# Outputs of two attention heads in the two halves of one PSUM bank, evicted together

## The chip, the cores and the metric

The kernel runs on one core of a Trainium2 chip. The metric is the device time of one execution in microseconds (us). The kernel before takes 481.25 us, the median of 3 runs (481.04 to 482.96). The kernel after is measured in the same way.

## The reference

One decoder layer on x of 256 tokens by 1024 channels, in float32, with a condition vector c:

```
mod = silu(c) @ w_ada + b_ada                      # 1024 -> 6 x 1024: sh1, sc1, g1, sh2, sc2, g2
h = rms_norm(x, g_pre_mix) * (1 + sc1) + sh1
proj = h @ w_in                                    # q, k, v of 16 heads, index heads, gates
o_sb = stick_breaking_attention(q, k, v)           # 6 heads of 64
o_mb = moba_attention(...)                         # 5 heads: at 256 tokens a causal softmax with ALiBi
o_ds = dsa_attention(...)                          # 5 heads: the 64 best keys of each query by an indexer
g = sigmoid(gate_logits + b_gate)
y = (g_sb * (o_sb @ w_proj_sb) + g_mb * (o_mb @ w_proj_moba) + g_ds * (o_ds @ w_proj_dsa)) @ w_o
x = x + g1 * rms_norm(y, g_post_mix)
h = rms_norm(x, g_pre_ffn) * (1 + sc2) + sh2
y = (silu(gate) * up) @ w_down                     # SwiGLU, 2816 wide
x = x + g2 * rms_norm(y, g_post_ffn)
```

For a head, with scores z of 256 queries by 256 keys, softmax heads form exp(z - max) / sum and stick-breaking heads exp(z + sums over later keys of log(1 - sigmoid(z))), both causal, and multiply the result with v. That product is 64 channels by 256 tokens.

## The kernel before, in words

**Precision.** The large products are made of two cuts of each operand: a high part (`whi`, `hhi`, `ohi`: ScalarE copies the float32 value to fp32r) and the rest (`wlo`, `hlo`, `olo`: VectorE subtracts the high part). `three` issues high*high, high*low and low*high (L1198 to L1200). So each weight that arrives by DMA in `raw` is cut by ScalarE (L611) and then by VectorE (L877) before TensorE uses it.

**The unit loop.** The product of h with `w_in` is divided into 51 units, numbered u = 0 to 50, by `mix_units`. A unit is one TensorE accumulation over 8 chunks of 128 channels into bank 0 or 1 (`unit`), taken out by ScalarE (`take_unit`). Units 27 to 50 are gates. Units of one weight block share its cuts: units 27 to 30 are block 11, 31 to 34 block 12, 35 to 38 block 13, and so on. A block is cut in quarters, listed in `PIECES_AT` at the units of the block before.

Everything else of the stage is hung on unit numbers. Each engine runs the same loop over u, and at each u the steps that are due, in program order. Semaphores join the engines. For head n (0 to 4 moba, 5 to 10 stick-breaking, 11 to 15 dsa):

- `SCORES_AT`, unit 13 + 2n: TensorE makes z. The two heads of a pair are made together (`TOGETHER_AT`), a pair being heads 0-1, 2-3, 5-6, 7-8, 9-10, 11-12, 13-14. Heads 4 and 15 are single.
- `EXP_AT`, one unit later: for a softmax head the exponential on ScalarE; for a stick-breaking head three ScalarE steps (L710 to L712), one on VectorE (L1037) and a triangular mask on GpSimd (L551).
- `NORM_AT`, two units later: VectorE normalises a softmax head.
- `SECOND_AT`, three units later (`second`): a softmax head's probabilities are turned by TensorE into bank 4 (`B_T`); for a stick-breaking head the sums over later keys are added to z, ScalarE takes the exponential into `buft` (L748) and GpSimd masks it (L543).
- `OUTPUT_AT`: TensorE multiplies `buft` with v (`output`). Heads with even number within their branch land on PSUM partitions 0 to 63, odd ones on 64 to 127. ScalarE writes `ohi` (L740), VectorE the rest (L1015).

**Other work in the loop.** `LOGITS_AT` are the indexer's logits (units 5 to 12) in banks 2 to 5. `ROUND_AT` (units 25 to 32) are VectorE's 8 rounds of top-8. The modulation rows 1 and 2 (`w_ada`) come by GpSimd's DMAs, VectorE multiplies and adds them up (`accumulate`, L946), TensorE sums over partitions (`sum_acc`) and turns the row (`turn_rows`), and VectorE forms columns (`columns`, which ends with an increment of `col_ready`, L933): group 1 at units 24, 25 and 26, group 2 at units 48, 49 and 50.

**PSUM banks before.** 0 and 1: units. 2 to 5: logits and scores (`z_place`: heads 0 to 4 in 2 and 3; stick-breaking heads h in 2 + h % 4, so that head 8 is in bank 5; dsa heads in 5, 4, 2, 3, 2). 4: turned probabilities. 5 (`B_ADA`): modulation sums and the indexer's turned weights. 6 and 7 (`B_O`): outputs, bank 6 + n % 2. The turned sums of groups 0, 1, 2 are in banks 7, 5, 4 (`B_ROWS`).

**After the loop.** Each branch's output is projected, gated by VectorE, added up by GpSimd (L581, L584), cut, multiplied with `w_o`, normalised, and then the SwiGLU stage runs over 11 steps of 256 hidden channels. The order of all this is written out by hand; no planner is involved.

Of the kernel before, what the change touches and what calls it, by code (L numbers as in the profile page):

```python
# [19 lines left out]
F32 = mybir.dt.float32  # L20
F32R = mybir.dt.float32r
ALU = mybir.AluOpType
ACT = mybir.ActivationFunctionType
AX_X = mybir.AxisListType.X

P = 128
D = 1024
KC = D // P
S = 256
# [213 lines left out]
def decoder_layer(nc, x, c, w_ada, b_ada, g_pre_mix, g_post_mix, w_in, b_gate, w_proj_sb,  # L243
                  w_proj_moba, w_proj_dsa, w_o, g_pre_ffn, g_post_ffn, w_up, w_down, out):
    ctx = ExitStack()
    with ctx:
# [74 lines left out]

        psum = ctx.enter_context(nc.psum_tensor("psum", [P, 8, BANK], F32))
        bank = [psum[:, i, :] for i in range(8)]
        B_UNIT, B_Z, B_T, B_ADA, B_O = 0, 2, 4, 5, 6
        B_ROWS = (7, B_ADA, B_T)
        B_Y = ((6, 0), (4, 6))
        B_TURNED = (2, 4)
        B_UP = ((2, 3), (0, 1))
# [264 lines left out]
        def _(act):  # L593
# [103 lines left out]
            for u in range(N_UNITS):  # L697
# [23 lines left out]
                if u in EXP_AT and EXP_AT[u] in SOFT_NO:  # L721
# [12 lines left out]
                                             scale=SLOPES[2 * h + (branch == "ds")],  # L734
                                             bias=smax[:, n % 2, t:t + 1], accum_out=ssum[:, n % 2, t:t + 1])
                    ins.then_inc(exp_ready, 1)
                for n in OUTPUT_AT.get(u, ()):
                    p0, ch = HD * (HEADS[n][1] % 2), O_CHUNK[HEADS[n][0]][HEADS[n][1]]
                    act.wait_ge(o_ready, n + 1)
                    act.activation(ohi[p0:p0 + HD, ch, :], bank[B_O + n % 2][p0:p0 + HD, 0:S], ACT.Copy).then_inc(o_hi, 1)  # L740
                if u in SECOND_AT:
                    n = SECOND_AT[u]
                    if n >= 2:
# [114 lines left out]
        def _(dve):  # L858
# [56 lines left out]
            def columns(g):  # L915

                dve.wait_ge(m_turned, g + 1)
                m, first, second = col[g][:, :], col[g][:, 0:KC], col[g][:, KC:2 * KC]
                bias = VEC_ADA + 2 * KC * g
                turned_sums = bank[B_ROWS[g]][:, :].rearrange("p (c j r) -> p j c r", c=4, j=4)[:, :, :, 0]  # L920

                then(dve.tensor_tensor(m.rearrange("p (j c) -> p j c", j=4), vecs[:, bias:bias + 2 * KC].rearrange("p (j c) -> p j c", j=4),
                                       turned_sums, ALU.add if g == 0 else ALU.subtract))

                if g == 0:
                    ins = dve.scalar_tensor_tensor(second, second, 1.0, vecs[:, VEC_PRE_MIX:VEC_PRE_MIX + KC], ALU.add, ALU.mult)
                elif g == 1:
                    ins = dve.tensor_tensor(first, first, vecs[:, VEC_POST_MIX:VEC_POST_MIX + KC], ALU.mult)
                else:
                    then(dve.scalar_tensor_tensor(first, first, 1.0, vecs[:, VEC_PRE_FFN:VEC_PRE_FFN + KC], ALU.add, ALU.mult))  # L930
                    ins = dve.tensor_tensor(second, second, vecs[:, VEC_POST_FFN:VEC_POST_FFN + KC], ALU.mult)
                then(ins)
                dve.sem_inc(col_ready, 1)  # L933
# [54 lines left out]
            for u in range(N_UNITS):  # L988
# [7 lines left out]
                if u in LOGITS_AT:  # L996
# [5 lines left out]
                    for t, (c0, c1) in enumerate(((0, P), (P, CAUSAL))):  # L1002
# [4 lines left out]
                            ins = dve.scalar_tensor_tensor(score[:, c0:c1], bufp[h % 2][:, c0:c1], w, score[:, c0:c1],  # L1007
                                                           ALU.mult, ALU.add)
                        ins.then_inc(score_added, 1)
                for n in OUTPUT_AT.get(u, ()):  # L1010
                    p0, ch = HD * (HEADS[n][1] % 2), O_CHUNK[HEADS[n][0]][HEADS[n][1]]
                    dve.wait_ge(o_hi, n + 1)

                    lo = olo[p0:p0 + HD, ch, :] if ch < FULL_OCH else ohi[HD:P, ch, :]
                    dve.tensor_tensor(lo, bank[B_O + n % 2][p0:p0 + HD, 0:S],  # L1015
                                      ohi[p0:p0 + HD, ch, :].bitcast(F32), ALU.subtract).then_inc(o_lo, 1)
                if u in NORM_AT and NORM_AT[u] in SOFT_NO:

                    n = NORM_AT[u]
# [175 lines left out]
        def _(pe):  # L1195
# [38 lines left out]

            def turn_rows(g):
                pe.wait_ge(m_ready, g + 1)
                if g == 2:
                    pe.wait_ge(pt_ready, N_SOFT)
                for n in range(4):
                    mm = pe.transpose(bank[B_ROWS[g]][:, P * n:P * (n + 1)], mrow[:, P * n:P * (n + 1)], ident[:, :])  # L1240
                mm.then_inc(m_turned, 1)

            def spread_gain(i):
# [59 lines left out]
            def scores(together):  # L1303
                for n in together:
                    m = Z_BEFORE[n]
                    if m is None:
                        pe.wait_ge(relu_ready, H_IX)
                    elif m in SB_NO:
                        pe.wait_ge(a_ready, SB_NO[m] + 1)
                    else:  # L1310
                        pe.wait_ge(max_ready, SOFT_NO[m] + 1)
                    if z_place(n) == B_T:
                        pe.wait_ge(pt_ready, softs_before(SB_FIRST))
                    elif z_place(n) == B_ADA:
                        pe.wait_ge(col_ready, 2)
                made = []
                for n in together:
                    _, h, tq, tk, _ = HEADS[n]
# [23 lines left out]
            def output(heads):  # L1342

                for n in heads:
                    if n in SB_NO:
                        pe.wait_ge(a_masked, 2 * (SB_NO[n] + 1))
                    else:
                        pe.wait_ge(pt_ready, SOFT_NO[n] + 1)
                    if n >= 2:
                        pe.wait_ge(o_lo, n - 1)  # L1350
                for keys in range(2):
                    for n in heads:
                        h, v0 = HEADS[n][1], HEADS[n][4]
                        p0, a = HD * (h % 2), buft[n % 2]
                        dst, cols = bank[B_O + n % 2][p0:p0 + HD, :], slice(v0 + HD * h, v0 + HD * (h + 1))
                        if keys == 0:
                            pe.matmul(dst[:, 0:S], v[:, 0, cols], a[:, 0:S], start=True, stop=False, skip_group_check=True)  # L1357
                        else:
# [11 lines left out]
            for u in range(N_UNITS):  # L1370
# [12 lines left out]
                if u in LOGIT_PAIR_AT:  # L1383
                    j = LOGIT_PAIR_AT[u]
                    if j == 0:
                        pe.wait_ge(unit_read, 5)
                        pe.wait_ge(vec_ready, 1)
                    if j == 1:
                        pe.wait_ge(wix_ready, 1)
                    if j >= 2:  # L1390
                        pe.wait_ge(relu_ready, 2 * (j - 1))
                    query_major([(bank[B_Z + h % 4], qk[:, T_QIX + h // 2, :], qk[:, T_KIX, :], HD * (h % 2))
# [183 lines left out]
```

## Time and profile before

| | |
|---|---|
| median of 3 runs | 481.25 us |
| the profiled execution | 479.4 us |
| its span (first to last instruction) | 477.7 us |
| mean granted TensorE clock | 0.988 of full speed |
| TensorE matmuls busy | 443.4 us, 93% |
| VectorE busy | 325.6 us, 68% |
| ScalarE busy | 242.8 us, 51% |
| GpSimd busy | 58.5 us, 12% |
| DMA | 98.79 MB, mean 207 GB/s |

The profile is one execution, seen by the hardware profiler. Its durations and gaps belong to its own 479.4 us, not to the median. A busy share is a mean over stages that have different limits: the head of the kernel, up to 30 us, waits for DMA; the unit loop lasts until about 225 us; the merge of the branches until about 262 us; the rest is the product with `w_o` and the SwiGLU stage. Matmuls are pipelined, so a row's duration is longer than the distance to the next row's start.

### The profile page before, as it was taken

The numbers are of one execution on the slowest core, as the hardware profiler recorded it, in microseconds if no ns is written. First come the engines' busy times: TensorE is split into PE (matmuls) and PEld (weight loads), VectorE is DVE, ScalarE is ACT, GpSimd is POOL, SyncE is SP. The second block draws the span as 40 slices with busy tenths as digits, with TensorE's granted clock in tenths as the row PEclk, the third lists the DMA queues.
The fourth block names the chain that finished last, engine by engine and source line by source line (L and its number), as shares of the span: only waits on it lengthen the run. The fifth ranks groups of instructions, "written<-read, shape, count | busy, mean of one in ns | idle before, by whom it ended". The sixth has DMA issues, their size and how long they took to land.

```text
span 477.7 us, 7668 instructions
## 1 busy us (share of the span) xinstructions
PE 443.4 (93%) x2933; PEld 388.9 (81%) x2933; DVE 325.6 (68%) x529; ACT 242.8 (51%) x426; POOL 58.5 (12%) x96
## 2 busy tenths in 40 slices
PE   0959999999989998999998899999999999999994
PEld 0529999999978998998987699888888888888883
DVE  2047678879599969793789656786855775595545
ACT  5046546556666755757457337653544253344332
POOL 2001002100024130002587200000000000000000
PEclk9959999999999999999999999999999999999999
DMA  8997897597865574742656920898475556630002
GB/s 302 424 357 221 296 326 239 181 325 248 282 232 169 218 265 150 266 159 66 200 188 240 365 88 1 281 363 273 142 247 190 169 182 184 236 107 0 2 0 88
DMA packets 56369, 98.79 MB, mean 207 GB/s; under 512 B 5036, under 2 KB 41492, under 8 KB 53268
## 3 DMA queue, kind: packets, MB, share of 16 engines
q1 hardware_dynamic: 54036, 81.62, 49.7%
q0 software_dynamic: 2304, 16.78, 10.0%
q8 instruction: 19, 0.31, 0.3%
q14 instruction: 10, 0.08, 0.1%
HBM read 97.35 MB, written 1.05 MB: 206 GB/s over the span
## 4 chain that ended last, share of the span: by engine, by line
PE 77%; DMA 6%; DVE 6%; ACT 4%; issue 3%; POOL 2%; SPq 1%; DVEq 0%; ACTq 0%; POOLq 0%; PEldq 0%
PE psum L1508 16%; PE psum L1198 15%; PE psum L1200 14%; PE psum L1199 14%; PE psum L1509 8%; DMA ada_end<-in_w_ada_dram 4%; PE psum L1472 3%; DVE wlo L877 3%; DMA raw<-in_w_o_dram 2%; ACT whi L611 2%; PE psum L1357 1%; PE psum L1294 1%; PE psum L1292 1%; POOL xn L584 1%; PE psum L1328 1%
## 5 line engine op out<-in xcount | busy, mean ns | idle before, releaser
L1508 PE MATMUL psum<-hcut,whi 128*128 128x512 f32 x320 | 111.8, 394 | 0.0
L1198 PE MATMUL psum<-hcut,whi 128*128 128x256 f32 (+1 forms) x360 | 105.8, 294 | 4.0 <-DVE hcut L981 2.7
L877 DVE TENSOR_TENSOR wlo<-raw,whi 128x1024 fp32r<-128x1024 f32 (+4 forms) x92 | 91.7, 1026 | 22.2 <-ACT whi L611 21.9
L1199 PE MATMUL psum<-hcut,whi 128*128 128x256 f32 (+1 forms) x360 | 102.2, 284 | 0.0
L1200 PE MATMUL psum<-hcut,wlo 128*128 128x256 f32 (+1 forms) x360 | 102.2, 284 | 0.0
L1509 PE MATMUL psum<-hcut,wlo 128*128 128x256 f32 x320 | 88.8, 278 | 0.0
L611 ACT ACTIVATE whi<-raw 128x1024 fp32r<-128x1024 f32 (+4 forms) x92 | 74.3, 842 | 17.6 <-DMA raw<-in_w_in_dram 15.6
L1198 PEld LDWEIGHTS psum<-hcut,whi 128*128 128x128 f32 (+1 forms) x360 | 68.8, 191 | 9.0 <-issue 4.3
L1508 PEld LDWEIGHTS psum<-hcut,whi 128*128 128x128 f32 x320 | 60.0, 188 | 14.1 <-issue 0.2
L1199 PEld LDWEIGHTS psum<-hcut,whi 128*128 128x128 f32 (+1 forms) x360 | 69.0, 192 | 0.0
L1200 PEld LDWEIGHTS psum<-hcut,wlo 128*128 128x128 f32 (+1 forms) x360 | 68.8, 191 | 0.0
L1509 PEld LDWEIGHTS psum<-hcut,wlo 128*128 128x128 f32 x320 | 60.1, 188 | 0.3
L1127 DVE TENSOR_TENSOR dlo<-draw,dhi 128x2048 fp32r<-128x2048 f32 x11 | 25.1, 2292 | 44.1 <-ACT dhi L786 44.1
L1122 DVE TENSOR_TENSOR wlo<-raw,whi 128x1024 fp32r<-128x1024 f32 x40 | 47.1, 1221 | 4.5 <-ACT whi L779 4.5
L779 ACT ACTIVATE whi<-raw 128x1024 fp32r<-128x1024 f32 x40 | 39.8, 1047 | 3.1 <-PE psum L1509 3.1
L786 ACT ACTIVATE dhi<-draw 128x2048 fp32r<-128x2048 f32 x11 | 20.9, 1911 | 31.2 <-PE psum L1200 31.2
L824 ACT ACTIVATE fsil<-fsil 128x256 f32<-128x256 f32 x20 | 8.4, 418 | 52.8 <-DVE fsil L1139 52.8
L946 DVE SCALAR_TENSOR_TENSOR acc<-xn,csil,acc 128x2048 f32<-128x2048 f32 x14 | 32.9, 2352 | 3.2 <-DMA xn<-in_w_ada_dram 3.1
L1198 PE MATMUL psum<-dhi,fhi 128*128 128x512 f32 x88 | 34.5, 392 | 0.0
L1200 PE MATMUL psum<-dhi,flo 128*128 128x512 f32 x88 | 34.4, 391 | 0.0
L1199 PE MATMUL psum<-dlo,fhi 128*128 128x512 f32 x88 | 34.3, 389 | 0.0
L1198 PE MATMUL psum<-whi,hcut 128*128 128x320 f32 (+2 forms) x80 | 28.6, 358 | 3.2 <-issue 2.2
(169 smaller groups left out, 692.1 us busy)
## 6 DMA issues: line engine op xcount, KB each, us to landing
raw<-in_w_up_dram SPq DMA_DIRECT2D x22, 1024.0 KB, 7.6
xn<-in_w_ada_dram POOLq DMA_DIRECT2D x16, 1024.0 KB, 5.2
raw<-in_w_in_dram SPq DMA_DIRECT2D x7, 2048.0 KB, 9.4
draw<-in_w_down_dram SPq DMA_DIRECT2D x11, 1024.0 KB, 5.1
raw<-in_w_in_dram SPq DMA_DIRECT2D x4, 1280.0 KB, 7.1
raw<-in_w_in_dram SPq DMA_DIRECT2D x3, 1536.0 KB, 7.2
raw<-in_w_ada_dram SPq DMA_DIRECT2D x2, 2048.0 KB, 9.6
ada_end<-in_w_ada_dram SPq DMA_DIRECT2D x4, 1024.0 KB, 16.8
```

The source lines that it names most:

```text
L611: act.activation(block_view(whi[b % 2], b)[0:p, chunks, cols], block_view(raw[r % 2], b)[0:p, chunks, cols], ACT.Copy).then_inc(w_hi, 1)
L779: act.activation(block_view(whi[slot], B_FFN)[:, 2 * q:2 * q + 2, :], block_view(raw[slot], B_FFN)[:, 2 * q:2 * q + 2, :], ACT.Copy).then_ ...
L786: act.activation(dhi[slot][:, :, :], draw[slot][:, :, :], ACT.Copy).then_inc(d_hi, 1)
L877: dve.tensor_tensor(block_view(wlo[b % 2], b)[0:p, chunks, cols], block_view(raw[r % 2], b)[0:p, chunks, cols], block_view(whi[b % 2], b)[ ...
L946: ins = dve.scalar_tensor_tensor(acc[:, :], ada_part, csil[:, k:k + 1], acc[:, :], ALU.mult, ALU.add)
L1122: dve.tensor_tensor(block_view(wlo[slot], B_FFN)[:, 2 * q:2 * q + 2, :], block_view(raw[slot], B_FFN)[:, 2 * q:2 * q + 2, :], block_view(w ...
L1127: dve.tensor_tensor(dlo[slot][:, :, :], draw[slot][:, :, :], dhi[slot][:, :, :].bitcast(F32), ALU.subtract).then_inc(d_lo, 1)
L1198: pe.matmul(dst, a[0], b[0], start=first, stop=False)
L1199: pe.matmul(dst, a[0], b[1], start=False, stop=False)
L1200: return pe.matmul(dst, a[1], b[0], start=False, stop=last)
L1508: pe.matmul(dst[:, :], wh, hcut[:, k, :, :].rearrange("p a s -> p (a s)"), start=k == 0, stop=False)
L1509: mm = pe.matmul(dst[:, S:2 * S], wl, hhi[:, k, :], start=False, stop=k == KC - 1)
```

## The change

The outputs of both heads of a pair go to bank 6, the even head to partitions 0 to 63 and the odd one to 64 to 127, as before within each bank. One ScalarE instruction and one VectorE instruction then handle 128 partitions. Single heads (4 and 15) keep 64 partitions. TensorE's `output` waits once for `o_lo` of all heads ahead. Bank 7, no longer an output bank, becomes `B_ADA`: modulation sums, the indexer's turned weights and all turned sums are there. Bank 5 holds logits and scores alone, and the waits that guarded its double use are gone.

```diff
-        B_UNIT, B_Z, B_T, B_ADA, B_O = 0, 2, 4, 5, 6
-        B_ROWS = (7, B_ADA, B_T)
+        B_UNIT, B_Z, B_T, B_O, B_ADA = 0, 2, 4, 6, 7
...
-                for n in OUTPUT_AT.get(u, ()):
-                    p0, ch = HD * (HEADS[n][1] % 2), O_CHUNK[HEADS[n][0]][HEADS[n][1]]
-                    act.wait_ge(o_ready, n + 1)
-                    act.activation(ohi[p0:p0 + HD, ch, :], bank[B_O + n % 2][p0:p0 + HD, 0:S], ACT.Copy).then_inc(o_hi, 1)
+                if u in OUTPUT_AT:
+                    heads = OUTPUT_AT[u]
+                    parts, ch = HD * len(heads), O_CHUNK[HEADS[heads[0]][0]][HEADS[heads[0]][1]]
+                    act.wait_ge(o_ready, heads[-1] + 1)
+                    act.activation(ohi[0:parts, ch, :], bank[B_O][0:parts, 0:S], ACT.Copy).then_inc(o_hi, len(heads))
...
-                turned_sums = bank[B_ROWS[g]][:, :].rearrange("p (c j r) -> p j c r", c=4, j=4)[:, :, :, 0]
+                turned_sums = bank[B_ADA][:, :].rearrange("p (c j r) -> p j c r", c=4, j=4)[:, :, :, 0]
...
-                for n in OUTPUT_AT.get(u, ()):
-                    p0, ch = HD * (HEADS[n][1] % 2), O_CHUNK[HEADS[n][0]][HEADS[n][1]]
-                    dve.wait_ge(o_hi, n + 1)
-
-                    lo = olo[p0:p0 + HD, ch, :] if ch < FULL_OCH else ohi[HD:P, ch, :]
-                    dve.tensor_tensor(lo, bank[B_O + n % 2][p0:p0 + HD, 0:S],
-                                      ohi[p0:p0 + HD, ch, :].bitcast(F32), ALU.subtract).then_inc(o_lo, 1)
+                if u in OUTPUT_AT:
+                    heads = OUTPUT_AT[u]
+                    parts, ch = HD * len(heads), O_CHUNK[HEADS[heads[0]][0]][HEADS[heads[0]][1]]
+                    dve.wait_ge(o_hi, heads[-1] + 1)
+
+                    lo = olo[0:parts, ch, :] if ch < FULL_OCH else ohi[HD:P, ch, :]
+                    dve.tensor_tensor(lo, bank[B_O][0:parts, 0:S], ohi[0:parts, ch, :].bitcast(F32),
+                                      ALU.subtract).then_inc(o_lo, len(heads))
...
                 pe.wait_ge(m_ready, g + 1)
-                if g == 2:
-                    pe.wait_ge(pt_ready, N_SOFT)
                 for n in range(4):
-                    mm = pe.transpose(bank[B_ROWS[g]][:, P * n:P * (n + 1)], mrow[:, P * n:P * (n + 1)], ident[:, :])
+                    mm = pe.transpose(bank[B_ADA][:, P * n:P * (n + 1)], mrow[:, P * n:P * (n + 1)], ident[:, :])
...
                     if z_place(n) == B_T:
                         pe.wait_ge(pt_ready, softs_before(SB_FIRST))
-                    elif z_place(n) == B_ADA:
-                        pe.wait_ge(col_ready, 2)
...
                         pe.wait_ge(pt_ready, SOFT_NO[n] + 1)
-                    if n >= 2:
-                        pe.wait_ge(o_lo, n - 1)
+                if heads[0]:
+                    pe.wait_ge(o_lo, heads[0])
...
-                        dst, cols = bank[B_O + n % 2][p0:p0 + HD, :], slice(v0 + HD * h, v0 + HD * (h + 1))
+                        dst, cols = bank[B_O][p0:p0 + HD, :], slice(v0 + HD * h, v0 + HD * (h + 1))
...
-                    if j == 1:
-                        pe.wait_ge(wix_ready, 1)
```

## Rows read from the trace of the kernel before

**Rows 1.** The page's chain that ended last: shares of the span by engine.

```profile
PE 77%; DMA 6%; DVE 6%; ACT 4%; issue 3%; POOL 2%; SPq 1%; DVEq 0%; ACTq 0%; POOLq 0%; PEldq 0%
```

**Rows 2.** TensorE's waits, 140 to 225 us: who <- for whom: total us, times, longest.

```profile
PE psum L1198 <- DVE wlo L877: 0.7, 1, 0.7
PE psum L1339 <- DVE smax L1052: 0.6, 1, 0.6
PE psum L1357 <- POOL buft L543: 0.6, 1, 0.6
```

**Rows 3.** TensorE's timeline: start, us, line, out<-in, count, idle before and releaser.

```profile
138.87 0.70 PE L1298 MATMUL psum<-qk 64*128 64x256 f32 x4 [1.86 <-DVEq L933]
```

**Rows 4.** VectorE's timeline, 138 to 149 us.

```profile
138.50 0.17 DVE L928 TENSOR_TENSOR col<-col,vecs 128x8 f32<-128x8 f32 x1
...
141.39 1.22 DVE L877 TENSOR_TENSOR wlo<-raw,whi 128x1024 fp32r<-128x1024 f32 x1
142.53 0.55 DVE L1037 SCALAR_TENSOR_TENSOR bufp<-psum,bufa 128x384 f32<-128x384 f32 x1
...
144.43 2.40 DVE L946 SCALAR_TENSOR_TENSOR acc<-xn,csil,acc 128x2048 f32<-128x2048 f32 x1
146.75 1.30 DVE L877 TENSOR_TENSOR wlo<-raw,whi 128x1024 fp32r<-128x1024 f32 x1
148.52 0.88 DVE L1015 TENSOR_TENSOR olo<-psum,ohi 64x256 fp32r<-64x256 f32 x2 [0.47 <-ACT ohi L740]
```

**Rows 5.** GpSimd's masks, the output waiting for one, VectorE beside the last.

```profile
137.02 0.54 POOL L551 TENSOR_SCALAR_AFFINE_SELECT bufp<-bufp 128x128 f32<-128x128 f32 x2 [0.71 <-DVE bufp L1037]
144.39 2.59 POOL L543 TENSOR_SCALAR_AFFINE_SELECT buft<-buft 128x128 f32<-128x128 f32 x2 [6.83 <-ACT buft L748]
147.23 0.65 PE L1357 MATMUL psum<-buft,v 128*64 128x256 f32 x4 [0.62 <-POOL buft L543]
...
160.00 0.55 DVE L1037 SCALAR_TENSOR_TENSOR bufp<-psum,bufa 128x384 f32<-128x384 f32 x1
160.37 0.53 POOL L543 TENSOR_SCALAR_AFFINE_SELECT buft<-buft 128x128 f32<-128x128 f32 x2 [0.58 <-ACT buft L748]
```

**Rows 6.** The chain in order of time: output of heads 7 and 8.

```profile
162.57 0.58 PE psum L1357 x4
```

**Rows 7.** Timeline: VectorE's last quarter of block 12, and TensorE reaching it.

```profile
150.86 1.22 DVE L877 TENSOR_TENSOR wlo<-raw,whi 128x1024 fp32r<-128x1024 f32 x1
...
154.04 0.28 PE L1198 MATMUL psum<-hcut,whi 128*128 128x256 f32 x1
```

**Rows 8.** Instructions of lines 740, 1015, 656: duration ns min/median/max, starts.

```profile
L740 ACT ACTIVATE ohi<-psum x16: 365/379/382, 105.3 to 219.7; 64x256 fp32r<-64x256 f32 x16
L1015 DVE TENSOR_TENSOR olo<-psum,ohi x14: 406/422/428, 105.7 to 209.7; 64x256 fp32r<-64x256 f32 x14
L656 ACT ACTIVATE qk<-psum x18: 371/385/386, 41.5 to 118.7; 128x256 f32<-128x256 f32 x18
```

**Rows 9.** Timeline after the output of heads 9 and 10.

```profile
179.09 0.88 DVE L1015 TENSOR_TENSOR olo<-psum,ohi 64x256 fp32r<-64x256 f32 x2 [1.02 <-ACT ohi L740]
...
182.34 0.52 PE L1339 MATMUL psum<-ident,bufp 128*128 128x128 f32 x3 [0.63 <-DVE smax L1052]
...
185.75 0.36 PE L1198 MATMUL psum<-hcut,whi 128*128 128x256 f32 x1 [0.74 <-DVE wlo L877]
```

**Rows 10.** Column tiles: a pair, the modulation sums, the single head; one record's duration.

```profile
118.55 0.65 PE L1357 MATMUL psum<-buft,v 128*64 128x256 f32 x4
...
217.83 1.06 PE L1231 MATMUL psum<-acc,neg 128*32 128x512 f32 x8
218.83 0.65 PE L1357 MATMUL psum<-buft,v 128*64 128x256 f32 x2
...
L1231 PE MATMUL psum<-acc,neg x16: 592/605/617, 123.3 to 218.3; 128*32 128x512 f32 x16
```

**Rows 11.** The chain in order of time: the load of `w_o`.

```profile
242.12 8.71 DMA raw<-in_w_o_dram
```

## The prediction

> **What bounds the kernel now.** I read the chain of waits first. TensorE holds 77% of it and VectorE 6% [rows 1]: the kernel is a sequence of matrix products, and another engine matters only where TensorE stands still for it. So the second view is the list of TensorE's own waits in the stage that the change touches, the mixer's unit loop (60 to 225 us of the span). Between 140 and 225 us it has three entries: 0.7 us for `wlo`, 0.6 us for `smax`, 0.6 us for `buft` [rows 2]. Ahead of them is a longer one, the product at 138.87 us, idle 1.86 us before, released by VectorE's sequencer at L933 [rows 3]. L933 is `sem_inc(col_ready)`, the end of `columns(1)`. Third, I read the timelines of VectorE and GpSimd around these four places, since TensorE can only gain where both are early enough.
>
> **Part 1: bank 5 is free of modulation sums.** Before, bank 5 held the summed modulation row of group 1, and scores of heads 7 and 8 (one of them in bank 5) waited in `scores` until `columns(1)` had run. The last of its instructions stands at 138.50 us [rows 4], and TensorE goes on at 138.87 [rows 3]. After, sums and turned sums live in bank 7, which no scores use, and the wait is gone. What else do these scores wait for? The index heads' relu and the softmax heads' `pt_ready`, both many units old; so they can follow unit 27 at once. Gain: 1.86 us. Below that lies zero, if another operand of unit 28 or of `second(6)` is late. Unit 28 uses the weight block of unit 27, already cut. `second(6)` needs GpSimd's mask of `bufp`, which starts at 137.02 and takes 0.54 us [rows 5]; `second(6)` now comes after scores and unit 28, which end well after 140 us. Neither holds it. I take 1.86 us.
>
> The other waits that the diff takes out (the logits' wait for `wix_ready`, `turn_rows(2)`'s for the last `pt_ready`, the scores' wait for head 11) show no idle time of TensorE anywhere in the lists, so they are worth nothing. `turn_rows`, `rows` and `columns` keep their instructions and only change banks; their order against each other is kept by `m_ready` and `col_ready` as before. No DMA is added, removed or moved in program order.
>
> **Part 2: what the earlier TensorE meets.** Everything after 138.87 us now comes 1.86 us earlier on TensorE, and ScalarE follows it, because its waits there are for TensorE. VectorE does not: it has hardly a gap up to its 0.47 us wait at 148.52 us [rows 4].
>
> First, the mask of `buft` for head 6, on which TensorE's output of heads 5 and 6 waited 0.62 us [rows 5]. Its two instructions began at 144.39 and took 2.59 us, while the same two began at 160.37 and took 0.53 us [rows 5]. The difference is what VectorE ran: a 2.40 us L946 from 144.43 with two SBUF tensors in [rows 4], against L1037 from 160.00, which reads PSUM and one SBUF tensor [rows 5]. Moved by 1.86 us, the mask begins at 142.53. There VectorE ends the L877 of 141.39 (1.22 us, until 142.61) and then runs L1037 (142.53 in the record) and the top-8 work until 144.43 [rows 4], none of which takes two SBUF tensors. So the mask should be done by about 143.2, and TensorE wants it at 147.23 - 0.62 - 1.86 = 144.75. The wait goes: 0.62 us more. If the mask stays 2.59 us long it keeps the whole wait: zero. It would become worse only if it slid behind a second long VectorE instruction. I take 0.62, and say openly that it is a matter of 1.3 us of phase.
>
> The Trainium skill (SBUF — State Buffer, "Who interferes with whom") says that a VectorE instruction with two SBUF inputs contends with a GpSimd instruction that reads SBUF, and one with at most one SBUF input, outside the two-port modes, doesn't. The trace agrees, 2.59 against 0.53 us; without the rule the mask's length would be chance, and the sum would be 0.62 us smaller.
>
> Second, the same contention can now hit the mask for head 8: it moves from 160.37 to 157.89, where VectorE is in accumulation and cutting. At the worst length seen near, 2.59 us, it ends at 160.48, and the output of heads 7 and 8 wants it at 162.57 [rows 6] - 2.48 = 160.09. That costs up to 0.4 us, at best nothing; I take nothing, since the row of 2.59 us began at the very start of a long instruction.
>
> Third, VectorE's cuts. TensorE's first unit of weight block 12 reaches the last quarter at 154.04 us [rows 7], after the change at 151.56. VectorE cuts that quarter in the L877 of 150.86 [rows 7]. It comes 0.47 us earlier because ScalarE's `ohi` is no longer late, and 0.44 us earlier by part 3, so it ends at 149.95 + 1.22 = 151.17. It fits by 0.4 us. Here a small new wait is nearest.
>
> **Part 3: two evictions become one, seven times.** Seven pairs of heads had two ScalarE copies of 64x256, 0.379 us each, and two VectorE subtractions, 0.422 us each [rows 8]. A ScalarE copy of 128x256 takes 0.385 us [rows 8], so the full height costs no more than half of it; VectorE's one I take at its 64x256 time, with 0.35 and 0.6 us as wide bounds. ScalarE gets back 7 x 0.37 = 2.6 us and VectorE 7 x 0.42 to 0.46 = 3.1 us, but in time of engines that are not the bound. It reaches TensorE where the chain runs through them: after the output of heads 9 and 10. There L1015 starts at 179.09 and takes 0.88 us for two; behind it in VectorE's order stand the normalisation, L1048, L1050 and L1052, for which the transposes at 182.34 waited 0.63 us, and then one accumulation and the L877 for which unit 39 waited 0.74 us at 185.75 [rows 9]. One subtraction less starts both 0.46 us earlier. The first wait shrinks from 0.63 to 0.17; the second stays 0.74, as TensorE and VectorE both come 0.46 earlier. Gain 0.46 us, not 0.92. With a 0.6 us subtraction it is 0.28 us. The other six pairs save nothing on TensorE beyond part 2, as no wait stands behind them.
>
> What speaks against merging is that ScalarE's copy of the first head no longer overlaps the wait for the second. Both heads' products end together already (four records of L1357 in 0.65 us), so that costs under 0.1 us of ScalarE.
>
> **Part 4: two heads write one bank.** The output products of a pair run on two column halves of the array. Pair: four records in 0.65 us; the single last head: two records, also 0.65 us [rows 10]. So halves run side by side now, in different banks. In one bank the nearest rows are the modulation sums, four column tiles of bank 5: eight records of 605 ns in 1.06 us [rows 10]; one after the other they would take 4.8 us. I take zero. The other end is a full single-head output more for each pair, 0.65 + about 0.2 us, 7 times: 5.6 us. The waits on `o_lo` ask for all heads ahead, as before: heads 5 and 6 are written at 147.23 [rows 5] and read until 149.40 [rows 4], the next pair is written at 162.57 [rows 6]. The alternation of two banks hid nothing.
>
> **Sum.** -1.86 - 0.62 - 0.46 = -2.9 us. Does it survive to the end? After 190 us no wait of TensorE stands in the list [rows 2]. The next stage is a chain of ScalarE, VectorE and GpSimd with the 8.71 us load of `w_o` that starts at 242.12 [rows 11], and each link is released by the one before, the load too (VectorE's cut frees its buffer), so the whole chain moves. The feed-forward part is TensorE's. The profiled execution took 479.4 us (span 477.7 and 1.7 around it), so it becomes 476.5. It was 1.85 us faster than the median shown; against 481.25 I predict 478.3 us.
>
> **Rivals.**
> A. Only the bank wait goes, and phases of VectorE and GpSimd take back the rest (the mask stays blocked, or block 12's last quarter is late): -1.9 + up to 0.3, about 479.5 us. For it: VectorE is full there, margins are 0.4 and 1.3 us. Against: both margins come out positive.
> B. The time goes into new waits almost wholly: unit 31, the mask of head 8, then unit 35 wait for a VectorE that was the true bound between 126 and 167 us. About -0.5 us, 480.8. For it: VectorE's 0.47 us gap is its only one for 20 us. Against: TensorE waited for none of its cuts there, with 2 us of room.
> C. More than forecast: VectorE's relief and unblocked masks also shorten the 0.74 us wait at 185.75. -3.7 us, 477.5.
> D. Slower: two column halves in one bank don't run side by side. Place: L1357 and L1359 in all seven pairs; +5.6 - 2.9 = +2.7 us, 484.0. It decides as soon as a pair costs 0.42 us more than now. Against it the 1.06 us of the sums; for it only that these use explicit 32-wide tiles.
>
> **Chances.** Forecast 0.50, A 0.22, B 0.12, C 0.10, D 0.06. Within 0.5% (2.4 us, about what a measurement tells from no change) begins at 478.85. The forecast lies 0.55 us under it, so I give it three quarters for faster; with C and a fifth of A that is 0.54. Same: a quarter of the forecast, the rest of A, and B, 0.40. Slower 0.06. The range 476.9 to 481.0 holds forecast, A, C and most of B; D is left out.
>
> **What would show it.** Right: no idle time before the scores of heads 7 and 8 (L1298); the mask of `buft` for head 6 around 142.5 us takes under 0.8 us and L1357 has no wait behind GpSimd; the wait before the transposes near 179 us is about 0.2 us; seven ScalarE and VectorE evictions of 128x256 at 0.39 and 0.42 us; four records of L1357 within 0.65 us. Wrong: L1357 pairs of 1.1 us or more (D); a new wait of unit 31 or 35 on `wlo` L877, or of L1357 on `buft` (A, B).

## The result, and the profile after

| | before | after |
|---|---|---|
| median, first measurement (8 runs each) | 480.38 us | 476.34 us |
| ratio, 95% interval | | 0.9925 (0.9900 to 0.9951) |
| median, second measurement (30 and 7 runs) | 479.68 us | 476.53 us |
| ratio, 95% interval | | 0.9951 (0.9933 to 0.9968) |
| profiled execution, span | 479.4, 477.7 us | 475.68, 473.9 us |
| VectorE busy, instructions | 325.6 us, 529 | 320.8 us, 522 |
| ScalarE busy, instructions | 242.8 us, 426 | 239.0 us, 419 |
| TensorE busy | 443.4 us | 443.1 us |

The change makes the kernel faster, by 0.5 to 0.75% by the two ratios. The medians differ by 4.04 us in the first measurement and 3.15 us in the second. The eight runs of before in the first are the three of the 481.25 us and five more, and the median of those five is 479.71 us, 3.4 us above the kernel after. The forecast was 478.3 us in a range from 476.9 to 481.0. The time lies 0.6 us below the range: the direction is right, the number is not.

TensorE did the same work as before. First TensorE's waits of the kernel after, 140 to 225 us, to be held against [rows 2]; from 120 to 140 us, where [rows 3] stood, the list is empty:

```profile
PE psum L1199 <- issue: 0.8, 1, 0.8
PE psum L1199 <- DVE wlo L877: 0.7, 1, 0.7
```

The 0.8 us belongs to the first product of the merge, at 222.69 us; before, the same one stands at 226.82, just outside the window. So of four waits in the lists one is left, the 0.74 us for `wlo`. Now TensorE's timeline around the other three (lines have moved by one to three: L1297 is the scores' product, L1354 and L1356 the output, L1336 the transposes):

```profile
135.76 0.28 PE L1201 MATMUL psum<-hcut,wlo 128*128 128x256 f32 x1
135.97 0.70 PE L1297 MATMUL psum<-qk 64*128 64x256 f32 x4
...
143.64 0.65 PE L1354 MATMUL psum<-buft,v 128*64 128x256 f32 x4
...
178.22 0.52 PE L1336 MATMUL psum<-ident,bufp 128*128 128x128 f32 x3
...
181.63 0.35 PE L1199 MATMUL psum<-hcut,whi 128*128 128x256 f32 x1 [0.74 <-DVE wlo L877]
```

None but the last has a bracket. Scores and output start 0.21 us behind the product ahead of them, as they do where nothing is waited for. The transposes start 0.38 us behind (178.22 against 177.84), before 0.91; at the other heads it is 0.12. So two waits are gone and the third has shrunk from 0.63 to 0.10 us of idle time, too short for a bracket. Laying TensorE's records of both kernels beside each other, one by one, gives the difference of their starts. It moves only in steps:

```
place                          before    after   after - before   step
unit 1                          38.34    37.39       -0.95
scores of heads 7, 8           138.87   135.97       -2.90       -1.95
output of heads 5, 6           147.23   143.64       -3.59       -0.69
transposes of head 11          182.34   178.22       -4.12       -0.53
first product of the merge     226.82   222.69       -4.13
first w_up product, second cut 299.55   295.56       -3.99
```

Between the steps it holds to a few hundredths for up to 100 us. To compare kernels I use one length: from the first index-logits product to the first product of the merge. It is 173.53 us before and 170.35 us after, -3.18 us. Repeating both kernels unchanged gave 173.51 and 170.38. So this length has a spread of some 0.03 us where medians of the same kernel differ by 1 us: the kernel before, run again beside itself, came to 480.66 against 479.68 us (ratio 1.0022, 0.9999 to 1.0044).

### The profile page after: what moved, and what is told of

The parts are those of the page before. It is cut to its first block, busy times and chain, and to the rows that moved or that the text cites. A ratio compares the mean times of both kernels' runs of the same rounds, so it can differ in the third digit from the quotient of the medians.

```text
span 473.9 us, 7659 instructions
## 1 busy us (share of the span) xinstructions
PE 443.1 (93%) x2933; PEld 388.5 (82%) x2933; DVE 320.8 (68%) x522; ACT 239.0 (50%) x419; POOL 56.7 (12%) x96
## 3 DMA queue, kind: packets, MB, share of 16 engines
q0 software_dynamic: 2304, 16.78, 10.2%
## 4 chain that ended last, share of the span: by engine, by line
PE 82%; DMA 6%; DVE 4%; ACT 3%; POOL 2%; issue 2%; SPq 1%; DVEq 0%; ACTq 0%; POOLq 0%; PEldq 0%
PE psum L1199 17%; PE psum L1503 16%; PE psum L1201 15%; PE psum L1200 15%; PE psum L1504 8%; DMA ada_end<-in_w_ada_dram 4%; PE psum L1467 3%; DMA raw<-in_w_o_dram 2%; DVE wlo L877 2%; ACT whi L610 1%; PE psum L1354 1%; PE psum L1293 1%; PE psum L1291 1%; PE psum L1325 1%; POOL xn L583 1%
## 5 line engine op out<-in xcount | busy, mean ns | idle before, releaser
L877 DVE TENSOR_TENSOR wlo<-raw,whi 128x1024 fp32r<-128x1024 f32 (+4 forms) x92 | 91.4, 1024 | 23.6 <-ACT whi L610 23.2
L946 DVE SCALAR_TENSOR_TENSOR acc<-xn,csil,acc 128x2048 f32<-128x2048 f32 x14 | 32.9, 2349 | 6.0 <-DMA xn<-in_w_ada_dram 5.9
```

What stands on the lines that cost most here:

```text
L877: dve.tensor_tensor(block_view(wlo[b % 2], b)[0:p, chunks, cols], block_view(raw[r % 2], b)[0:p, chunks, cols], block_view(whi[b % 2], b)[ ...
L946: ins = dve.scalar_tensor_tensor(acc[:, :], ada_part, csil[:, k:k + 1], acc[:, :], ALU.mult, ALU.add)
```

## The experiments

**Bank alone.** Both heads in bank 6, sums in bank 7, evictions separate.

```diff
-                if u in OUTPUT_AT:
-                    heads = OUTPUT_AT[u]
...
+                for n in OUTPUT_AT.get(u, ()):
...
+                    act.activation(ohi[p0:p0 + HD, ch, :], bank[B_O][p0:p0 + HD, 0:S], ACT.Copy).then_inc(o_hi, 1)
...
```

> The kernel after with its evictions taken apart again: both heads of a pair in bank 6, two ScalarE copies and two VectorE subtractions of 64x256. I measure the unit loop in the profile, from TensorE's first product of unit 1 to its first product of the merge: 188.48 us before, 185.30 us after. Theory (three separate steps: bank wait 1.95, mask 0.69, merged eviction 0.53): the first two remain, 185.8 us, with no idle time ahead of the scores of heads 7 and 8, a mask of head 6 under 0.8 us, and again about 0.6 us idle ahead of the transposes of head 11. Against before -2.6 us. Rival (shorter evictions are what lets VectorE follow the earlier TensorE): unit 31 then waits for its last weight quarter, since VectorE ends that 0.44 us later with a margin of 0.4, and the loop is 186.1 us or more. Second rival (the gain sits in the merged eviction): 188 us.

Measured: 477.11 us, ratio 0.9928 (0.9908 to 0.9948). The loop is 186.07 us from unit 1 (171.11 by the length above), between the theory's 185.8 and the rival's 186.1. TensorE's list shows the `smax` wait back at 0.62 us, as the theory says. The steps against before are -1.95, -0.69 and then +0.25, inside unit 31 at 151.60 us. There VectorE is late with its last quarter:

```profile
150.18 1.27 DVE L876 TENSOR_TENSOR wlo<-raw,whi 128x1024 fp32r<-128x1024 f32 x1
```

It ends at 151.45, and TensorE is waiting:

```profile
151.60 0.36 PE L1197 MATMUL psum<-hcut,whi 128*128 128x256 f32 x1
151.79 0.28 PE L1198 MATMUL psum<-hcut,whi 128*128 128x256 f32 x1
```

The first starts 0.31 us behind the one before it (151.29) and the second 0.19 us behind it, where 0.12 is usual: 0.25 us together. So the rival's mechanism is real and its size 0.25 us. The first merged pair, 5-6, takes exactly this away: in the kernel after the same cut ends at 149.85 us and TensorE comes to it at 150.45.

**Merging alone.** Sums stay in bank 5 with all waits.

```diff
-        B_UNIT, B_Z, B_T, B_O, B_ADA = 0, 2, 4, 6, 7
+        B_UNIT, B_Z, B_T, B_ADA, B_O = 0, 2, 4, 5, 6
+        B_ROWS = (7, B_ADA, B_T)
...
```

> The kernel before with merged evictions alone: both heads in bank 6 and evicted together, modulation sums still in bank 5, with all of its waits. Theory: the 1.86 us ahead of the scores of heads 7 and 8 and the 0.62 us for the mask of head 6 stay, the 0.63 us ahead of the transposes of head 11 becomes 0.17. Loop 187.9 to 188.0 us against 188.48 before. Rival (evictions matter in all seven pairs, ScalarE and VectorE being nearly full): 186.5 us or less.

Measured: 478.28 us, ratio 0.9963 (0.9946 to 0.9980). The 1.86 us wait stays, the transposes' shrinks to 0.10 us, as in the kernel after. But in the profiled execution the length is 174.07 us, longer than before. The windows (us, busy time and count of TensorE, of its weight loads, VectorE, ScalarE and GpSimd, granted clock, DMA share, GB/s) show why:

```profile
138.00:142.00 4.00, 4.00 (x21) 3.73 (x22) 3.93 (x9) 1.54 (x3) 0.00 (x0) 0.57 1.02 380
142.00:146.00 4.00, 4.00 (x32) 3.73 (x32) 3.87 (x9) 1.91 (x3) 0.95 (x1) 1.00 0.34 128
```

From the end of its 1.86 us gap to 141.5 us TensorE had its lower level of clock, 1.2 GHz, and it fell back by 1.55 us. The profile of before, with the same gap, has 1.00 throughout: 27 records from 138 to 142 us against 21 here. TensorE, later by this, waited only 0.17 us for the mask. So the length of this run can't say what merging saves. Its steps can: at the transposes of head 11 the difference to before moves by -0.53 us, as in the kernel after. The median, 2.2 us under before, is more than that explains. How much merging alone is worth in the median stays open.

**The mask and the accumulation.** In the kernel before, one accumulation a unit earlier.

```diff
-ADA_UNIT = [2, 4, 6, 9, 12, 15, 18, 22, 25, 28, 31, 34, 37, 40, 43, 46]
+ADA_UNIT = [2, 4, 6, 9, 12, 15, 18, 22, 25, 27, 31, 34, 37, 40, 43, 46]
```

> The kernel before, with one step of the modulation work (VectorE's accumulation L946 of unit 28) at unit 27. Nothing else is changed. Theory (GpSimd's mask is held up by a VectorE instruction with two SBUF inputs): at 144.39 us the accumulation is over, the two mask instructions of head 6 take 0.5 to 1.2 us instead of 2.59, and the 0.62 us wait of the output of heads 5 and 6 is gone: loop 187.8 us against 188.48. The 1.86 us bank wait stays. Rival (the mask's length comes from GpSimd itself or from ScalarE's late exponential): the mask still takes about 2.6 us or the wait stays at 0.62, loop 188.5 us.

Measured: 479.44 us, ratio 0.9976 (0.9959 to 0.9994). Length 172.82 us, -0.71. The first line is GpSimd's mask here, the second VectorE's accumulation:

```profile
144.31 0.68 POOL L543 TENSOR_SCALAR_AFFINE_SELECT buft<-buft 128x128 f32<-128x128 f32 x2
...
141.11 2.35 DVE L946 SCALAR_TENSOR_TENSOR acc<-xn,csil,acc 128x2048 f32<-128x2048 f32 x1
```

0.68 us against the 2.59 of [rows 5] at the same time of the kernel, and the `buft` wait is no longer in the list. The mask overlaps the end of an L877 (two SBUF tensors, until 144.60) and then L1037 (one). What VectorE runs decides the mask's length; the rival falls.

**The last wait: four kernels.** First the accumulation of unit 37 alone goes behind the last cut of block 14.

```diff
-ADA_UNIT = [2, 4, 6, 9, 12, 15, 18, 22, 25, 28, 31, 34, 37, 40, 43, 46]
+ADA_UNIT = [2, 4, 6, 9, 12, 15, 18, 22, 25, 28, 31, 34, 38, 40, 43, 46]
```

> The kernel after, with the accumulation of unit 37 at unit 38, behind the cut of the last quarter of weight block 14. Theory (the 0.74 us wait of unit 39 is the length of VectorE's queue, in which 2.35 us of accumulation stand ahead of that cut): the wait goes and the loop takes 184.4 us against 185.30 after. Rival (ScalarE's high cut of that quarter or the load is late too): wait and loop unchanged, 185.3 us. The time of the whole kernel 0.9 us under the kernel after.

Measured: 477.29 us, ratio 0.9936 (0.9918 to 0.9955), length 171.23 against 170.35. The 0.74 us wait went, and a wait of 1.58 us for `bufp` came at 194.90 (VectorE idle for 3.94 us, until 190.37, for the next modulation load). Both theory and rival miss: the wait was VectorE's queue, but the move broke something else. Then the followers move too:

```diff
-ADA_UNIT = [2, 4, 6, 9, 12, 15, 18, 22, 25, 28, 31, 34, 37, 40, 43, 46]
+ADA_UNIT = [2, 4, 6, 9, 12, 15, 18, 22, 25, 28, 31, 34, 38, 41, 44, 46]
```

> The kernel after, with the accumulations of units 37, 40 and 43 at 38, 41 and 44. The earlier try moved one alone, and VectorE then waited 3.94 us for the next modulation part at 190 us, because its load started later. Here each load has three units again. Theory: the 0.74 us wait of unit 39 goes and nothing takes its place, unit loop 184.4 us against 185.30 after. Rival (a later accumulation always costs what it gives back, in another wait of TensorE on VectorE): 185.3 us or more, with a new wait between 186 and 218 us.

Measured: 476.95 us, ratio 0.9955 (0.9936 to 0.9974), length 170.66. The rival holds: at 196.26 us TensorE waits 1.04 us for `wlo`, as the accumulation of unit 41 now stands ahead of another last quarter. Then a finer place for the first, in unit 38 directly behind the cut:

```diff
                     cut_lo(b, q)
+                if u == 38:
+                    accumulate(ADA_AT[37])
...
-                if u in ADA_AT:
+                if u in ADA_AT and u != 37:
```

> The kernel after, in which VectorE makes the accumulation of unit 37 in unit 38, directly behind the cut of block 14's last quarter: 1.2 us later than now, not a whole unit later as in the two tries before. Both tries took the 0.74 us wait away and paid elsewhere: moved alone, the next part's load came late (VectorE idle 3.94 us); moved with its followers, the accumulation of unit 41 stood ahead of block 15's last quarter (1.04 us). Theory (what was wrong in them was the place, not the idea): the wait at about 181.6 us goes, no new one, unit loop 184.4 to 184.6 us against 185.30 and 185.33 after. Rival (the 1.2 us already delay the next part's load enough): VectorE waits at unit 40 and TensorE at unit 40 or 42, loop 185.3 us or more.

Measured: 477.18 us, ratio 0.9944 (0.9924 to 0.9965), length 171.25. The rival holds again, and VectorE's next accumulation says what is late:

```profile
189.74 2.35 DVE L946 SCALAR_TENSOR_TENSOR acc<-xn,csil,acc 128x2048 f32<-128x2048 f32 x1 [3.94 <-DMA xn<-in_w_ada_dram]
```

Its load was issued by GpSimd at 181.86 us and landed 7.9 us later. The two issues in the kernel after (first GpSimd's 1 MB, then SyncE's 2 MB load), and in this one:

```profile
180.64 0.55 POOL L526 DMA_DIRECT2D xn<-in_w_ada_dram  x1 [7.76 <-DVE acc L946]
181.56 0.37 SPq L434 DMA_DIRECT2D raw<-in_w_in_dram  x1
```

```profile
179.37 0.37 SPq L434 DMA_DIRECT2D raw<-in_w_in_dram  x1
181.86 0.55 POOL L526 DMA_DIRECT2D xn<-in_w_ada_dram  x1 [8.89 <-DVE acc L946]
```

SyncE's load of block 16 waits for block 14's last cut. Cutting first lets it overtake the modulation load, which waits for the accumulation. The fourth kernel turns the order back:

```diff
                         sp.wait_ge(w_lo, 4 * (b0 + 1))
+                        if b == 16:
+                            sp.wait_ge(w_lo, 4 * 15 + 1)
```

> The previous try (accumulation of unit 37 behind the last cut of block 14) with one wait more: SyncE issues the 2 MB load of block 16 only when VectorE has also cut the first quarter of block 15, about 3 us later. In the profile of that try SyncE issued this load at 179.37 us and GpSimd the 1 MB modulation load at 181.86, behind it, and VectorE then stood idle for the latter until 189.74; in the kernel after GpSimd issues at 180.64 and SyncE at 181.56, and VectorE doesn't wait. Theory (the order of the two loads is what made both tries fail): the modulation part is there when VectorE comes to it, near 186 us, no wait of 1.6 us ahead of the turned probabilities at 194 us, and the wait at 181.6 us is gone too: from the first index product to the first product of the merge 169.5 us against 170.35 and 170.38 in the kernel after. Whole kernel 0.8 us under after. Rival (the modulation load takes as long in either order, as it starts 1.2 us later): 171.2 us as in the try, or 170.4 if it costs just what it gives.

Measured: 475.03 us, ratio to before 0.9896 (0.9867 to 0.9924), the lowest median of all. Its interval is clear of that of the kernel after in the second measurement (0.9933 to 0.9968) and overlaps that of the first (0.9900 to 0.9951). The length is 169.40 us, 0.95 less than after, and the theory had 169.5. TensorE's list from 140 to 225 us keeps one entry:

```profile
PE psum L1203 <- issue: 0.8, 1, 0.8
```

The issues and the accumulation behind the loads:

```profile
182.87 0.37 SPq L436 DMA_DIRECT2D raw<-in_w_in_dram  x1
...
181.94 0.55 POOL L528 DMA_DIRECT2D xn<-in_w_ada_dram  x1 [8.88 <-DVE acc L948]
...
187.11 2.35 DVE L948 SCALAR_TENSOR_TENSOR acc<-xn,csil,acc 128x2048 f32<-128x2048 f32 x1 [1.23 <-DMA xn<-in_w_ada_dram]
```

Issued at the same time as in the kernel before it, the part lands 5.2 us later instead of 7.9. In the kernel after, where it also goes 0.9 us ahead, it took 5.2 us too. VectorE still waits 1.23 us, but that delays nobody.

**The gap and the clock.** First the gap of the kernel before is filled with 14 products.

```diff
+                if u == 27:
+                    pe.wait_ge(o_lo, 4)
+                    for k in range(14):
+                        pe.matmul(bank[B_O + 1][:, 0:S], block_view(whi[11 % 2], 11)[:, k % KC, 0:P], hhi[:, k % KC, :], start=True, stop=True)
```

> The kernel before, with 14 further products of 256 columns (a product of unit 27 repeated into the then idle output bank 7, the result never read) in front of the scores of heads 7 and 8. At 0.12 us each they take 1.7 us, nearly all of the 1.86 us in which TensorE stood idle there. The wait itself stays. Theory (in a part of its executions the kernel before also loses TensorE's clock in that gap, as the merge-only kernel's profile shows with a granted clock of 0.50 from 138 to 141.7 us, about 1.5 us lost): more work, but a shorter median, by 0.5 to 1 us against 480.4, mean granted clocks of its runs at 0.985 and above, and full clock after the gap in its profile. Rival (the clock is lost at the start only, where this changes nothing): median within 0.3 us of before or slower, and the same spread of clocks, 0.977 to 0.991.

Measured: 479.96 us, ratio 1.0015 (1.0000 to 1.0030), length 173.52. The median is not shorter, against the theory. Its clocks are higher (at 0.984 or below in 1 of 11 runs, before in 8 of the 30 beside it and in 8 of 12 of its repetition), but its profile is 1.06 us longer in the SwiGLU stage, where TensorE waits 0.90 us once for `wlo` L1122, a wait no other kernel has; I can't say why. With that in the way the run decides nothing. The other test lengthens the gap:

```diff
+                if u == 27:
+                    pe.wait_ge(w_lo, 4 * 12 + 1)
```

> The kernel before, in which TensorE waits ahead of the scores of heads 7 and 8 for one VectorE instruction more, the first cut of block 12, which ends at 140.04 us: the gap grows from 1.86 to about 3.2 us. Theory (a gap of TensorE here can cost its clock): the granted clock is 0.50 for some microseconds after it in the profile, and the median is longer by more than the 1.35 us of the wait, by 2 to 3 us. Rival (the drop to half in the merge-only kernel's profile had nothing to do with the gap): full clock, and 1.35 us longer: 481.0 to 481.8 us.

Measured: 481.80 us, ratio 1.0042 (1.0020 to 1.0063). The gap became 3.09 us. The windows before, in and behind the stretch at half clock:

```profile
136.00:139.00 3.00, 0.94 (x8) 0.73 (x7) 2.72 (x11) 1.42 (x2) 0.79 (x4) 1.00 0.93 353
140.00:143.00 3.00, 2.97 (x14) 2.58 (x15) 2.48 (x7) 1.23 (x3) 0.00 (x0) 0.50 1.03 380
143.00:146.00 3.00, 3.00 (x23) 2.73 (x22) 2.58 (x8) 0.79 (x2) 0.00 (x0) 0.96 0.41 158
```

Clock 0.50 right behind the gap, 14 records in 3 us against 23. The length, 175.48 us, is 1.95 longer than before: +1.23 of gap, +1.4 of clock, -0.7 because the mask's wait vanished. The mask took 1.03 us: it began at 146.97, 1.72 us into VectorE's accumulation, where before the two began together. Neither text foresaw the last term, which hides half of the clock's cost; the median lies at the rival's end, the profile is the theory's.

**One pair merged.** The kernel after, only heads 9 and 10 evicted together.

```diff
-                if u in OUTPUT_AT:
+                if u in OUTPUT_AT and (OUTPUT_AT.get(u) == (9, 10)):
...
```

> The kernel after with only the outputs of heads 9 and 10 evicted together; the other six pairs are in bank 6 too, but taken out by two ScalarE and two VectorE instructions each. Theory: of the 0.77 us that the bank-only kernel's unit loop (186.07 us) is longer than the kernel after (185.30), pair 9-10 is 0.53 and pair 5-6 the 0.18 us by which unit 31 missed its last weight quarter; the other five are nothing. So 185.5 us here, with no wait ahead of the transposes of head 11 beyond 0.2 us and a shift of 0.18 us inside unit 31. Rival (the six others count in full): 185.3 + 6/7 of 0.77 = 186.0 us.

Measured by its profile: unit 1 ran at half clock here, so 185.83 us contains 0.28 us of the start; by the length from the index logits it is 170.60, 0.25 more than after and 0.51 less than the bank-only kernel. All of it sits in unit 31, where the difference of starts rises by 0.25 us, as in the bank-only kernel; no other step follows. The transposes stand as in the kernel after. So pair 5-6 is worth 0.25 us (the theory had 0.18), pair 9-10 is 0.51 to 0.53, and the other five are nothing; the rival's 0.66 is out. This rests on one profile.

**Both kernels again.**

> The kernel before, unchanged, for a second profile and more runs. Theory (three waits, all set by program order): unit loop 188.48 us with 1.86, 0.62 and 0.63 us of idle again where the clock stays full, and about 1.5 us more where it falls to half in the first gap. All differences ahead of unit 1 are chance. Rival (the 0.95 us by which the kernel after was ahead at unit 1 is its own): unit 1 starts at 38.3 to 38.4 us again.

> The kernel after, unchanged, for a second profile and more runs. Theory: unit loop 185.3 us again with the single wait of 0.74 us; the start of unit 1 anywhere from 37.3 to 38.5 us, as in the five profiles so far. Rival (the start is the change's, by its sums in bank 7): unit 1 at 37.4 us again. The ratio to before 0.9925 within 0.002.

Measured: lengths as given above, with the same waits to 0.01 us (1.86, 0.62, 0.62 and 0.74; 0.74). Unit 1 starts at 38.55 us in the second profile of before and at 38.31 in that of after, not at 37.4 again, so the lead of 0.95 us in the first profile was not the change's. It goes with the clock at the start: from some 26 to 31 us on the granted clock is 0.50 for 6.8 us in seven of the fourteen profiles (the first of after among them), where unit 1 starts at 37.3 to 37.7 us, and for 10.2 us in the other seven, where it starts at 37.8 to 38.6. The ratio of after was 0.9951, 0.0026 from the first: outside the 0.002 that I had allowed.

## Why the prediction was wrong, and where it was right

**Part 1, bank 5: right, 1.95 us for 1.86.** Scores follow unit 27 at 0.21 us of the previous start (135.76 to 135.97), and `second(6)` and unit 28 had all they needed. The 0.09 us is in how a bracket is read: the idle time counts from the modelled end of the product before. From start to start the gap was 2.14 us (from 136.73), and 0.21 is usual. The same holds for the mask: 0.90 us from start to start, and 0.21 after.

**Part 2, the mask: right, 0.69 us for 0.62.** It was to start at 142.53 with TensorE 1.86 us earlier. With the 0.95 us of the start taken off the forecast is 141.58; it started at 141.49, and VectorE stood where [rows 4] put it:

```profile
141.49 0.56 POOL L542 TENSOR_SCALAR_AFFINE_SELECT buft<-buft 128x128 f32<-128x128 f32 x2 [4.90 <-ACT buft L748]
141.57 0.55 DVE L1038 SCALAR_TENSOR_TENSOR bufp<-psum,bufa 128x384 f32<-128x384 f32 x1
```

The moved accumulation shows the same in the kernel before, with nothing else changed. The Trainium skill (SBUF — State Buffer, "Who interferes with whom") gives the rule for it: a VectorE instruction with two SBUF inputs contends with a GpSimd instruction that reads SBUF. The runs agree with it, 2.59 us beside L946, 0.56 beside L1038.

The mask for head 8, which could have cost 0.4 us, took 0.68 us and cost nothing. The cut for unit 31 fitted, by 0.6 us where 0.4 was forecast, but only with the merged pair: without it TensorE lost 0.25 us.

**Part 3, the merged eviction: right, 0.53 us for 0.46.** The lines of evictions after:

```profile
L740 ACT ACTIVATE ohi<-psum x9: 363/384/385, 104.4 to 215.6; 128x256 fp32r<-128x256 f32 x7, 64x256 fp32r<-64x256 f32 x2
L1016 DVE TENSOR_TENSOR olo<-psum,ohi x7: 416/424/424, 104.9 to 205.3; 128x256 fp32r<-128x256 f32 x7
```

0.384 and 0.424 us for double the rows, against 0.379 and 0.422 [rows 8]: height costs nothing. The wait before the transposes shrank to 0.10 us where the forecast left 0.17; that is the difference between 0.46 and 0.53. "The other six pairs save nothing on TensorE beyond part 2" holds in its letter, since part 2 had counted on pair 5-6's 0.44 us; without it TensorE loses 0.25 us, by bank alone and one pair merged. So merging is worth 0.76 us on top of the bank's change (171.11 - 170.35), not 0.53. The 0.74 us wait stayed, as said.

**Part 4, one bank: right.** Four records of L1354 in 0.65 us, as in two banks [rows 10]. Rival D is out. Its price was also added up wrongly: 7 times 0.85 us is 5.95, not 5.6. And the chances for faster add up to 0.52, not 0.54; neither bears on the outcome.

**The sum.** Three terms were forecast at -2.94 us and measured at -3.17. The chain carried them through the merge to the end: from the first product of the merge to TensorE's last product it took 244.16 and 244.37 us before, 244.56 and 244.19 us after, the same within 0.4 us.

**What failed is the last step**, "against 481.25 I predict 478.3 us", and the range built on it. On the profiled execution the same sum gave 476.5 us (479.4 - 2.9), 0.2 us from the measured median of 476.34. The prediction saw that this execution was 1.85 us faster than the median of three runs, and still took those three as its reference. They lie high: the five further runs of the first measurement have a median of 479.71 us, and 84 runs of before beside the experiments 480.26. So of the miss of 1.96 us, 1.54 us is the reference (481.25 - 479.71), 0.23 us are the three terms, and 0.2 us is left, which is noise: the intervals of the two ratios mean 2.4 to 4.8 us and 1.5 to 3.2 us gained, and both hold the 3.17 us of the steps.

The range, 1.4 us below the forecast, was made of the margins of masks and cuts; the spread of the reference was put at nothing. The 84 single runs of before lie between 478.05 and 482.31 us, and one of the 12 of its repetition at 485.10.

That spread goes with the granted clock: 39 of the 84 runs with a mean clock up to 0.984 have a median of 480.7 us, 32 up to 0.989 have 479.8, and 13 above have 478.6. In the profiles the clock is at half in these places: from some 26 to 31 us on, where TensorE waits for the first weights; twice behind the gap ahead of the scores of heads 7 and 8; and in two profiles near the first `w_o` products, at 260 us. It is also at half for the last 3 to 6 us of every profile. The mean does not tell which: it is 0.988 in the profile of before, which otherwise lost clock at the start alone, and 0.988 in that of merge-only, which lost less there and the rest behind the gap.

The gap of [rows 3] is one such place, so part of what the change brings may be clock. Of all runs, those of kernels with that gap of 1.86 us lie at 0.984 or below in 50 of 113, those of kernels without it in 15 of 67, and with the gap lengthened 8 of 10. At 1.5 us for each such loss (1.55 and 1.4 measured) the difference in shares would be some 0.3 us for the change, an estimate. It is argued, not shown: the same kernel before lay there in 8 of 30 runs and in 8 of 12 beside them, the filled gap didn't give a shorter median, and merge-only, which has the gap, had no such run among 7.

Of the rivals' sums C's, 477.5 us, is the nearest, but by another route: the 0.74 us wait that it would have shortened was untouched.

## What to carry to other kernels

When a buffer serves two users, look for the wait that its double use makes, not at the instructions saved: here a bank's second user cost 1.95 us, and of seven evictions less on each of two engines one gave 0.53 us, one kept a new wait of 0.25 us away, and five gave nothing. A wait of the engine that sets the time, when it goes, is worth its start-to-start gap less the usual one, and it moves that engine against all others: recompute which masks, cuts and loads now meet. Before an instruction is moved in a full queue, ask which DMA its end releases and which other DMA then goes first. And forecast in the place where the change acts, where the profile is good to 0.03 us; take as reference for the whole time more than three runs, and give it a range that holds the spread of the kernel before.

## What the runs showed of the hardware

- GpSimd's two mask instructions of 128x128, 0.53 us with VectorE idle (175.95 us in before), took 0.68 us where they overlapped the last 0.3 us of a subtraction with two SBUF tensors, 2.59 us beside VectorE's accumulation, which reads two SBUF tensors and a scalar, and 3.54 us in the kernel after beside such an accumulation and a subtraction.
- A gap of TensorE of 3.09 us was followed by half clock (1.2 GHz) until 143.2 us, 1.4 us lost; gaps of 1.86 us were followed by full clock in three profiles (before twice, and with the accumulation moved) and by half clock in one.
- The same 1 MB load landed 5.2 us after its issue when it went 0.9 us ahead of a 2 MB load of another queue (in two kernels), and 7.9 us after when it went 2.5 us behind it (in two).
- ScalarE copies and VectorE subtractions out of PSUM took the same time for 64 and for 128 partitions.
- Two halves of the array's columns wrote one bank side by side: 0.65 us for the four records of a pair, in one bank as in two. Four tiles of 32 columns did so too: eight records of 0.6 us in 1.06 us [rows 10].
